# Window attention with the shifted value rows copied from two products instead of a third product, and the first scores put ahead of the second query product

## What is computed

```python
qkv = h @ w_qkv + b_qkv                       # 16 query heads, 4 key/value heads, 64 wide
q = qkv[..., :nq].reshape(b, n_c, CHUNK, SWA_KV_HEADS, g, SWA_HEAD_DIM)
k = _band(...)                                # for each chunk of 64 tokens: the chunk before and the chunk itself
v = _band(...)
logits = einsum('bcqkgd,bcskd->bckgqs', q, k) * scale + pos_bias
m = maximum(max(logits), sink)
p = exp(logits - m) / (sum(exp(logits - m)) + exp(sink - m))
o = einsum('bckgqs,bcskd->bcqkgd', p, v)
return o @ w_o + b_o
```

## Time and profile before

| | |
|---|---|
| median of 3 runs | 1166.26 us (1164.61 to 1167.34) |
| the profiled execution | span 1165.4 us; a time of its own beside the span is not given |
| TensorE busy | 1152.4 us, 99% of the span |
| VectorE / ScalarE / GpSimd busy | 804.1 / 633.8 / 273.5 us |
| layer 2's mixer on TensorE | from 595.16 us |

### The profile page before, as it was taken

One profiled execution on the slowest core, in us unless ns is written; L12 is line 12 of the kernel. 1 busy time (PEld: TensorE's weight loads), 2 busy tenths in 40 slices (PEclk: granted clock), 3 DMA queues, 4 the chain that ended last, 5 costly groups with the idle time before them and its releaser, 6 DMA issues.

```text
span 1165.4 us, 17759 instructions
## 1 busy us (share of the span) xinstructions
PE 1152.4 (99%) x7208; PEld 1026.1 (88%) x7208; DVE 804.1 (69%) x880; ACT 633.8 (54%) x753; POOL 273.5 (23%) x251
## 2 busy tenths in 40 slices
PE   9999999999999999999999999999999999999997
PEld 7999888888998888888899888888889998888886
DVE  6786877775688677767657777767646868776742
ACT  6676565563445556555435656555346765655632
POOL 2100532222123354221111344221110005322100
PEclk9999999999999999999999999999999999999999
DMA  9432555567563255555553355555554325555550
GB/s 355 150 118 73 217 185 196 198 168 238 181 207 118 84 191 196 181 184 194 197 184 117 128 191 181 184 192 199 184 181 167 123 73 217 184 194 199 195 186 37
DMA packets 31259, 202.34 MB, mean 174 GB/s; under 512 B 3552, under 2 KB 4640, under 8 KB 7760
## 3 DMA queue, kind: packets, MB, share of 16 engines
q1 hardware_dynamic: 28800, 196.88, 47.5%
q10 hardware_dynamic: 2032, 3.07, 1.0%
q0 software_dynamic: 352, 1.31, 0.8%
HBM read 198.43 MB, written 1.84 MB: 172 GB/s over the span
## 4 chain that ended last, share of the span: by engine, by line
PE 94%; DMA 2%; DVE 1%; POOL 1%; SPq 1%; issue 1%; ACT 1%; ACTq 0%; DVEq 0%; POOLq 0%
PE banks L1332 40%; PE banks L1336 21%; PE banks L1320 8%; PE banks L1326 6%; PE banks L1327 6%; PE banks L1328 6%; DMA raw<-w 2%; PE banks L1467 1%; PE banks L1404 1%; PE banks L1481 1%; PE banks L1623 1%; PE banks L1469 0%; SPq L319 0%; PE banks L1635 0%; POOL scratch L359 0%
## 5 line engine op out<-in xcount | busy, mean ns | idle before, releaser
L859 DVE TENSOR_TENSOR w_lo<-raw,w_hi 128x2048 fp32r<-128x2048 f32 x180 | 442.5, 2463 | 194.8 <-ACT w_hi L500 194.5
L500 ACT ACTIVATE w_hi<-raw 128x2048 fp32r<-128x2048 f32 x183 | 348.7, 1907 | 62.2 <-DMA raw<-w 23.5
L1332 PE MATMUL banks<-x_split,w_hi 128*128 128x512 f32 x1408 | 336.8, 391 | 0.0
L1332 PEld LDWEIGHTS banks<-x_split,w_hi 128*128 128x128 f32 x1408 | 258.5, 188 | 50.3 <-DVE w_lo L859 0.4
L1336 PEld LDWEIGHTS banks<-x_split,w_lo 128*128 128x128 f32 x1408 | 181.0, 191 | 7.1
L1336 PE MATMUL banks<-x_split,w_lo 128*128 128x256 f32 x1408 | 184.0, 283 | 0.0
L1332 PE MATMUL banks<-hid_split,w_hi 128*128 128x512 f32 x528 | 130.1, 392 | 1.4 <-DVE x L1279 1.4
L1332 PEld LDWEIGHTS banks<-hid_split,w_hi 128*128 128x128 f32 x528 | 95.5, 188 | 19.2 <-DVE x L1279 1.6
L1326 PE MATMUL banks<-x_split,w_hi 128*128 128x256 f32 x384 | 110.7, 288 | 0.0
L1327 PE MATMUL banks<-x_split,w_hi 128*128 128x256 f32 x384 | 109.4, 285 | 0.0
L1328 PE MATMUL banks<-x_split,w_lo 128*128 128x256 f32 x384 | 109.3, 285 | 0.0
(11 more groups left out here) (199 smaller groups left out, 1636.2 us busy)
## 6 DMA issues: line engine op xcount, KB each, us to landing
raw<-w SPq DMA_DIRECT2D x183, 1024.0 KB, 4.9
raw<-w SPq DMA_DIRECT2D x8, 256.0 KB, 6.0
x<-x_in SPq DMA_DIRECT2D x4, 256.0 KB, 5.4
raw<-w SPq DMA_DIRECT2D x2, 512.0 KB, 7.3
k_all<-k_all ACTq DMA_DIRECT2D x1, 960.0 KB, 8.0
rel_scratch<-rel_lut POOLq DMA_DIRECT2D x1, 768.0 KB, 9.9
rel_bias<-rel_scratch POOLq DMA_DIRECT2D x2, 256.0 KB, 9.0
y_gain<-final_rows ACTq DMA_DIRECT2D x1, 512.0 KB, 6.5
```

What stands on the lines that cost most here:

```text
L500: act.activation(w_hi[u % HI_SLOTS][:, :], raw[slot][:, :], ACT.Copy).then_inc(hi_done, 1)
L859: dve.tensor_tensor(w_lo[slot][:, :], raw[slot][:, :], w_hi[u % HI_SLOTS][:, :].bitcast(FP32), ALU.subtract).then_inc(lo_done, 1)
L1332: return pe.matmul(pair(b), wt[0], xs, start=first, stop=False, skip_group_check=True)
```

## The change

The third value product is gone, and with it the third single column of the RMS sums. VectorE's `windows()` writes, after each of the two value products, the full 128 rows and then half of them (64 rows) once more to the shifted window: tokens 64 to 127 from partitions 64 to 127 of bank 0 to partitions 0 to 63, and tokens 128 to 191 from partitions 0 to 63 of bank 1 to partitions 64 to 127. TensorE runs `logits(0)` straight behind the value products and `two_tiles(b+3)` behind it. VectorE runs `scores` and `inverse` of groups 0 and 1 before `over_rms(2)` and `split(b+6)`; ScalarE runs `exps(0)` and `exps(1)` before `split(b+6)` and `biased(2)`.

```diff
--- before.py
+++ after.py
@@ -78,7 +78,7 @@
 
 SHARED = 8 * HEADS * SEQ + 8 * D + 20 * SEQ
 
-TOKEN_SUMS = [3 if n == 4 else 2 if n in (0, 6) else 0 for n in range(NORMS)]
+TOKEN_SUMS = [2 if n in (0, 4, 6) else 0 for n in range(NORMS)]
 
 
 DOWN_EVENTS = sorted([(FFN_T * (t + 1), 0, t) for t in range(KT)] + [(16 * (j + 1), 1, j) for j in range(FFN_CHUNKS)])
@@ -717,10 +717,10 @@
                 biased(0)
                 biased(1)
                 split(b + 5)
+                exps(0)
+                exps(1)
                 split(b + 6)
                 biased(2)
-                exps(0)
-                exps(1)
                 split(b + 7)
                 exps(2)
                 biased(3)
@@ -1133,13 +1133,15 @@
                 def windows():
 
                     dve.wait_ge(bv_loaded, 16)
-                    for t in range(3):
-                        if t < 2:
-                            dve.wait_ge(m.v_part, t + 1)
+                    for t in range(2):
+                        if t == 0:
+                            dve.wait_ge(m.v_part, 1)
                         else:
                             dve.wait_ge(unit_used, b + 3)
-                        dst = v_all[:, t, 0:256] if t < 2 else v_all[:, 0, 256:512]
-                        dve.scalar_tensor_tensor(dst, bank[t][:, 0:256], rstd[:, SEQ + t:SEQ + t + 1], bv_rows[:, :],
+                        dve.scalar_tensor_tensor(v_all[:, t, 0:256], bank[t][:, 0:256], rstd[:, SEQ + t:SEQ + t + 1],
+                                                 bv_rows[:, :], ALU.mult, ALU.add).then_inc(m.v_new, 1)
+                        dve.scalar_tensor_tensor(v_all[own(t), 0, 256:512], bank[t][others(t), 0:256],
+                                                 rstd[others(t), SEQ + t:SEQ + t + 1], bv_rows[others(t), :],
                                                  ALU.mult, ALU.add).then_inc(m.v_new, 1)
 
                 def scores(g):
@@ -1182,12 +1184,12 @@
                 over_rms(1)
                 split(b + 5)
                 windows()
-                split(b + 6)
-                over_rms(2)
                 scores(0)
                 scores(1)
                 inverse(0)
                 inverse(1)
+                over_rms(2)
+                split(b + 6)
                 scores(2)
                 scores(3)
                 over_rms(3)
@@ -1360,7 +1362,7 @@
                     pe.wait_ge(one_loaded, 16)
                 pe.wait_ge(norm.ss, n + 1)
                 last = pe.matmul(bank[6][:, 0:SEQ], ones, ss[:, 0, :], start=True, stop=True)
-                for t, first in enumerate((0, P, CHUNK)[:TOKEN_SUMS[n]]):
+                for t, first in enumerate((0, P)[:TOKEN_SUMS[n]]):
                     last = pe.matmul(bank[6][:, SEQ + t:SEQ + t + 1], ss[:, 0, first:first + P], ones[:, 0:1],
                                      start=True, stop=True)
                 last.then_inc(norm.sums, 1)
@@ -1689,12 +1691,11 @@
 
                 u = b + 2
                 pe.wait_ge(lo_done, u + 1)
-                for t, first in enumerate((0, P, CHUNK)):
+                for t, first in enumerate((0, P)):
                     for k in range(KT):
                         xt = tuple(v[:, k, first:first + P] for v in (x_hi, x_lo))
                         last = moving_weights(bank[t][:, 0:256], w_tile(u, k, 256), xt, k == 0, k == KT - 1)
-                    last.then_inc(m.v_part if t < 2 else unit_used, 1)
-                two_tiles(b + 3, SWA_BANKS[2], x_tile)
+                    last.then_inc(m.v_part if t == 0 else unit_used, 1)
 
                 def place(g):
 
@@ -1755,13 +1756,14 @@
                     part(u, SWA_BANKS[t], x_tile, tiles)
 
                 logits(0)
+                two_tiles(b + 3, SWA_BANKS[2], x_tile)
                 pe.wait_ge(m.q_tmp, 3)
                 late_queries(3, range(0, 4))
                 logits(1)
                 late_queries(3, range(4, KT))
                 transposes(0)
                 transposes(1)
-                pe.wait_ge(m.v_new, 3)
+                pe.wait_ge(m.v_new, 4)
                 late_queries(4, range(0, 5))
                 logits(2)
                 late_queries(4, range(5, KT))
```

## The result

The changed kernel takes 1170.49 us in the median of 4 runs (1170.02 to 1171.31), against 1165.49 us of before in the same comparison: 5.0 us more, a ratio of 1.0042 with a 95% interval of 1.0031 to 1.0054. Two later comparisons gave 1.0033 (1.0020 to 1.0046) and 1.0034 (1.0022 to 1.0045). The profiled execution has a span of 1169.0 us; its own time was 1170.85 us, so 1.85 us lie around the span.

What follows compares the result with a forecast made beforehand. TensorE, busy 1152.4 of 1165.4 us, was taken as the bound. −3.1 removed + 5.1 wait + 0.1 start gave +2.1; with +1.5 for the clock, 1166.26 + 3.6 = 1169.9 us, range 1167.5 to 1171.5.

Steps and rivals of the forecast that it cites:

- The removal: TensorE, layer 2: third value product (−2.91 us) and one RMS-sum column (−0.20) go, −3.1 us; no wait at logits(0).
- VectorE's chain: Value rows 2.0 us, then 5.87 to over_rms(2): TensorE waits 5.1 us, query pair 2 starts 2.1 later.
- The clock: TensorE's clock falls to half behind the wait at query pair 2: +1.5 us; rival of it staying up, chance 0.17.
- the bounds of 0 to 3.0: Half clock's price behind query pair 2's wait: nothing, or twice 1.5 us; rival of a longer half clock, chance 0.10.
- Nothing given back: Behind query pair 2 in layer 2, the 1.0 us of waits stay; rival that they vanish: 1168.9, chance 0.10.
- The sum: Whole kernel: +2.1 and +1.5 us make +3.6; profiled span 1169.0, median 1169.9 us, chance 0.58.

Runs made afterwards that it cites:

- experiment 6: Changed kernel with TensorE's old order, value rows ahead of split(b+5), over_rms(2) ahead of all scores, scores(4), scores(5) earlier, ScalarE reordered: 1161.97 us, ratio 0.9963.
- experiment 9: Kernel before, third product kept, with scores(4) and scores(5) earlier on VectorE and ScalarE's later part reordered: 1165.13 us against 1166.03, ratio 0.9990.
- experiment 8: Changed kernel with its four value-row instructions ordered full, full, half, half: 1169.88 us in a single run.
- experiment 1: Removal alone: third product gone and shifted rows from VectorE, but all engines in the order of the kernel before: 1164.56 us against 1165.70, ratio 0.9990.
- experiment 2: Order alone: kernel before with its third product kept and the new order on the three engines: 1166.80 us against 1165.70, ratio 1.0010.
- experiment 4: Changed kernel with over_rms(2) directly behind the value rows, ahead of the scores, and biased(2) ahead of exps(0): 1167.14 us against 1165.70, ratio 1.0010.
- experiment 7: Changed kernel with over_rms(2) between the scores and inverses of groups 0 and 1, and biased(2) behind exps(1): 1166.26 us against 1165.99, ratio 1.0005.
- experiment 3: Changed kernel with 38 throw-away matmuls on TensorE ahead of the wait for over_rms(2): 1168.96 us against 1165.70, ratio 1.0031.
- experiment 11: Changed kernel with 38 throw-away matmuls in the wait, run beside the unfilled changed kernel: 1168.74 us against 1166.03 before, ratio 1.0017.
- experiment 5: Changed kernel run again as it is: 1169.86 us against 1165.99 before, ratio 1.0033.
- experiment 10: Changed kernel as it is, run beside the one with 38 throw-away matmuls: 1170.23 us against 1166.03 before, ratio 1.0034.

## Why the prediction was right

Measured +5.0, +3.9 and +4.2 us in three comparisons, forecast +3.6; 1170.49 us lies in the range. The forecast of 1169.9 us stood on 1166.26 us for the kernel before; from the 1165.49 us of the comparison it would be 1169.1, so that it came within 0.6 us is partly luck.

- **The removal.** Right: the value products end 5.84 us after their start, forecast 5.81, and no wait stands at `logits(0)`. That the product is worth 0.12 us a matmul and not the 0.28 that a matmul's row shows is seen in the trace (8.72 − 5.84 = 2.88 us for 24 matmuls) and in experiments 6 and 9 together (2.6 to 3.1 us).
- **VectorE's chain.** Right in its terms: value rows 2.05 us (2.0), 5.87 from `scores(0)` to `over_rms(2)` (5.87), wait 4.96 (5.1). Query pair 2 starts 18.07 us after the first value matmul, 15.73 before: +2.34, less the 0.20 of the sums, +2.1 as forecast. The 0.50 us of a value row was put together as 0.42 + 0.08; it is rather 0.39, the distance of two rows that are not held, and 0.12 for the hold (experiment 8). The sum is the same. Experiments 1, 2, 4 and 7 show that this wait is the loss: it stood at 1.50, 1.19, 0.78 and 2.27 us and was smaller wherever the order was partly undone. In experiment 7 the length moved with it one to one; in 4 part of it came back as another wait.
- **The clock.** That it falls was right, and experiments 3 and 11 show that the slow stretch comes from the wait: fill it and the stretch is gone, with `over_rms(2)` just as late. This term was too small for the first profile: 1.5 us forecast, 2.27 measured, and 1.49 and 2.35 in the two others (8.70 and 9.56 against 7.21 us). It counted the 16 slow matmuls of the one stretch in the trace of before; in the first profile all of the 24 in the first half of query pair 2 are slow, in experiment 5, where the clock fell later, some 16. The same wait costs different amounts, within the bounds of 0 to 3.0.
- **Left out.** `transposes(7)` starts 0.70 us behind `transposes(6)` instead of 0.44: 656.69 against 655.99. From `transposes(0)` to the last out-projections it is 30.42 us instead of 30.15. All kernels with four value-row instructions have it (experiments 1, 3 to 8, 10 and 11), those with three have not (before, 2 and 9). The weight load of `transposes(7)` waits for GpSimd's product of group 7, which follows VectorE's `inverse(7)`:

```profile
654.42 0.69 DVE L1173 TENSOR_REDUCE small<-scratch 128x4 f32<-128x512 f32 x1 [1.13 <-ACT small L700]
...
656.69 0.11 PEld L1729 LDWEIGHTS banks<-table,scratch 128*64 128x64 f32 x1 [0.34 <-POOL scratch L451]
```

That `inverse(7)` begins 0.45 us after ScalarE's line 700 has ended (653.97 to 654.42), in the kernel before 0.10 us (650.69 to 650.79); it is 0.45 or 0.46 in every profile with four value rows and 0.10 in every one with three. Why one VectorE instruction more has this effect so far behind is open.

- **Nothing given back.** Right: the three small waits are 0.24, 0.24 and 0.52 us in both profiles. Of the orders that were run, only those that bring `scores(4)` and `scores(5)` forward are without them (experiments 6 and 9).
- **The sum.** 2.14 + 2.27 + 0.27 = 4.7 for the length less the sums, which measured 4.88 − 0.20. The profiled executions' spans, 1165.4 and 1169.0, are only 3.6 apart because before's had lost 1.3 us more by the first value matmul (607.70 against 606.38), 0.2 of it the sums; it had the half clock in layer 0, the changed one had not. That the span agreed with the forecast's 1169.0 is partly luck.

## What to carry to other kernels

When the bounding engine sheds work, look at the instruction of another engine that it needs next. If that instruction comes no earlier, the gain turns into a wait, and whatever is put ahead of it lengthens the wait. Here the same removal was worth −1.1, +5.0 or, with the neighbours reordered too, −4.0 us. A long wait of TensorE also has to be priced with the half clock behind it, here 1.5 to 2.4 us behind 4.96 us, and removing it wins both.

## What the runs showed of the hardware

**Waits and the clock.** Waits of about the same length can be followed by a fall or not. In layer 1, TensorE waited 2.23 us in experiment 5 and 2.05 us in experiment 4. The first two rows are TensorE's timeline and clock in 5, the next two in 4:

```profile
275.18 3.47 PE L1334 MATMUL banks<-hid_split,w_hi 128*128 128x512 f32 x14 [2.23 <-DVE x L1281]
...
274.00:278.00 4.00, 2.82 (x12) 1.00 0.67 272
```

```profile
274.51 5.08 PE L1334 MATMUL banks<-hid_split,w_hi 128*128 128x512 f32 x14 [2.05 <-DVE x L1281]
...
274.00:278.00 4.00, 3.49 (x8) 0.57 0.61 252
```

The shorter one lost the clock. In the layer-2 stretches of the profiles, waits of 0.40 to 1.50 us never did (experiments 1 to 4 and 11), 2.00 and 2.27 did (4, 7), 4.83 did (8), and 4.96 did all three times. In layer 0 the wait at the RMS sums was followed by the half clock in four profiles (1.51 us before, 1.49, 1.48 and 1.47 in experiments 7, 9 and 10) and not in five others (1.47, 1.49, 1.63, 1.48 and 1.47 in experiments 1, 2, 4, 5 and 6): for waits of about 1.5 to 2.3 us their length does not tell, in these traces, whether the clock falls behind them. The Trainium skill, TensorE: Matmul & The Clock Gate, Part 1, has half rate as the default to which an idle engine falls back; the three falls behind 4.96 us agree.

**Instructions that begin on other partitions.** Two VectorE instructions of 0.48 us start 0.39 us apart when both begin on partition 0 and 0.50 to 0.53 apart when input or output begins on another one than last, whatever their height (experiment 8, and the four rows of the changed kernel). The Trainium skill, VectorE: DVE Perf Modes, section on two Vector instructions with no wait between them, gives such a hold; the rows agree with it.
